# Two transformer layers on one core: the per-group convolution table built in one piece, and one call that prepares weights early taken out

## The reference, cut to what matters

```python
def _conv_ffn(x, w_up, conv_w, conv_b, w_down):
    u = x @ w_up
    val, gate = u[..., :D_FF], u[..., D_FF:]            # D_FF = 2816 = 22 * 128
    gp = jnp.pad(gate, ((0, 0), (CONV_WIDTH - 1, 0), (0, 0)))
    h = conv_b + sum(gp[:, j:j + s] * conv_w[j] for j in range(CONV_WIDTH))
    return (jax.nn.silu(h) * val) @ w_down

def s5_mixer(h, ..., d_skip, w_glu):
    ...
    y = lax.map(scan_sequence, u)                        # 64 groups of 16 channels
    y = y + d_skip.reshape(SSM_GROUPS, SSM_GROUP) * u
    ...
```

## Time and profile before

| | |
|---|---|
| runs | 1783.55, 1789.47, 1784.94 us; median 1784.94 |
| the profiled execution | 1783.55 us, its span 1781.7 us |
| mean granted clock of TensorE | 0.992 |
| PE busy | 97% of the span |
| DVE, ACT, POOL busy | 45%, 38%, 40% |

### The profile page before, as it was taken

How to read it: one execution, slowest core, us unless ns; L and a number is a source line. 1 busy time by engine, 2 the same in 40 slices (tenths; PEclk the granted TensorE clock), 3 DMA queues, 4 the chain that set the end, 5 groups by cost and what they waited for, 6 DMA issues and landing times.

```text
span 1781.7 us, 22762 instructions
## 1 busy us (share of the span) xinstructions
PE 1734.6 (97%) x9006; PEld 1443.6 (81%) x9006; DVE 793.9 (45%) x1430; ACT 673.9 (38%) x1176; POOL 710.7 (40%) x331
## 2 busy tenths in 40 slices
PE   8999999999999898999999999999999999999999
PEld 6887977788788687789888888888888888888887
DVE  3876899678756547333111111148664411111111
ACT  3333344244243656433322222266654333122221
POOL 5432344444444231434453434333801244344342
PEclk9999999999999899999999999999999999999999
DMA  9422224453535457214333333222101233333332
GB/s 245 97 79 83 72 87 153 136 150 121 151 112 168 133 205 253 92 59 119 95 96 100 94 101 95 79 80 82 54 1 33 75 107 95 95 95 95 100 96 77
DMA packets 241288, 189.61 MB, mean 106 GB/s; under 512 B 40480, under 2 KB 198304, under 8 KB 241184
## 3 DMA queue, kind: packets, MB, share of 16 engines
q1 hardware_dynamic: 239312, 182.79, 34.4%
q10 hardware_dynamic: 1872, 5.37, 0.9%
HBM read 168.73 MB, written 19.40 MB: 106 GB/s over the span
## 4 chain that ended last, share of the span: by engine, by line
PE 83%; DVE 10%; ACT 3%; issue 2%; DMA 1%; POOL 1%; DVEq 0%; SPq 0%; ACTq 0%
PE ps L372 12%; PE ps L374 12%; PE ps L373 12%; PE ps L398 10%; PE ps L399 10%; PE ps L400 10%; PE ps L429 3%; PE ps L431 3%; PE ps L430 3%; PE ps L874 2%; PE ps L855 2%; PE ps L865 1%; DVE x_rows L1681 1%; PE ps L847 1%; ACT w_hi L1163 1%
## 5 line engine op out<-in xcount | busy, mean ns | idle before, releaser
L1013 POOL TENSOR_TENSOR w_lo<-w_raw,w_hi 128x1024 fp32r<-128x1024 f32 (+3 forms) x283 | 674.3, 2395 | 1010.2 <-ACT w_hi L1163 1010.2
L372 PE MATMUL ps<-a_hi,w_hi 128*128 128x512 f32 (+1 forms) x1184 | 442.8, 374 | 3.0 <-DVE ev L2003 3.0
L373 PE MATMUL ps<-a_lo,w_hi 128*128 128x512 f32 (+1 forms) x1184 | 441.1, 373 | 0.0
L374 PE MATMUL ps<-a_hi,w_lo 128*128 128x512 f32 (+1 forms) x1184 | 441.0, 372 | 0.0
L1163 ACT ACTIVATE w_hi<-w_raw 128x1024 fp32r<-128x1024 f32 (+3 forms) x283 | 283.2, 1019 | 212.8 <-DMA w_raw<-in_ffn_w_gate_up_dram 71.1
L372 PEld LDWEIGHTS ps<-a_hi,w_hi 128*128 128x128 f32 x1184 | 223.4, 189 | 43.6 <-DVE ev L2003 3.2
L374 PEld LDWEIGHTS ps<-a_hi,w_lo 128*128 128x128 f32 x1184 | 223.4, 189 | 39.0
L373 PEld LDWEIGHTS ps<-a_lo,w_hi 128*128 128x128 f32 x1184 | 223.4, 189 | 38.5
L2146 DVE TENSOR_TENSOR ev<-ps,xh 128x512 f32<-128x512 f32 x44 | 30.4, 692 | 411.9 <-PE ps L374 382.9
L398 PE MATMUL ps<-w_hi,h_hi 128*128 128x512 f32 x476 | 190.5, 400 | 7.2 <-DVE ev L2003 4.0
L399 PE MATMUL ps<-w_lo,h_hi 128*128 128x512 f32 x476 | 189.5, 398 | 0.0
(11 more groups left out here) (345 smaller groups left out, 2335.9 us busy)
## 6 DMA issues: line engine op xcount, KB each, us to landing
w_raw<-in_ffn_w_gate_up_dram SPq DMA_DIRECT2D x88, 512.0 KB, 3.8
w_raw<-in_w_up_dram SPq DMA_DIRECT2D x44, 512.0 KB, 4.1
w_raw<-in_ffn_w_down_dram SPq DMA_DIRECT2D x40, 512.0 KB, 3.7
w_raw<-in_w_in_dram SPq DMA_DIRECT2D x20, 512.0 KB, 4.3
w_raw<-in_w_down_dram SPq DMA_DIRECT2D x20, 512.0 KB, 4.4
s_records<-stage SPq DMA_DIRECT2D x16, 544.0 KB, 5.3
w_raw<-in_ssm_w_glu_dram SPq DMA_DIRECT2D x16, 512.0 KB, 4.2
rec<-s_records SPq DMA_DIRECT2D x14, 544.0 KB, 5.3
```

The lines of the kernel that those rows point to most:

```text
L372: pe.matmul(bank, wh, xh_, start=first, stop=False)
L373: pe.matmul(bank, wh, xl_, start=False, stop=False)
L374: return pe.matmul(bank, wl, xh_, start=False, stop=last)
L1013: pool.tensor_tensor(w_lo[:, n % RING, 0:w], w_raw[:, n % RING, 0:w], w_hi[:, n % RING, 0:w].bitcast(F), ALU.subtract).then_inc(lo_made, 1)
```

## The change

Three things change.

1. The four small products of `prepare` go to partitions 0 to 15 of the bank, side by side in its 512 columns, in place of four places 32 partitions apart. ACT copies the whole of it to `k_s` with one instruction of 16x4x128, which now frees the bank. DVE waits for that, multiplies the identity with `d_skip` for four groups at once into a scratch tile (16x64), waits for itself, adds it to the first 16 columns of `k_s` (16x4x16), and waits for that too. The eight passes on PE stay eight.
2. `d_skip` is loaded in another layout: two DMAs of 16x64 single numbers in place of four of 16x16.
3. The call at L1259 is gone: ACT makes chunks only 4 ahead.

```diff
-N_CONST, N_TURNED, N_PARAM = 13, 8, 7
+N_CONST, N_TURNED, N_PARAM = 13, 8, 5
...
-                b = open_bank(("s5k", f), freed_by=(k_w, f + 1))
+                b = open_bank(("s5k", f))
                 for g in range(GB):
-                    m = pe.matmul(b[KQ * g:KQ * g + GK, 0:P], h_bs[f % 2][:, g, T - 1, :],
+                    m = pe.matmul(b[0:GK, g * P:g * P + P], h_bs[f % 2][:, g, T - 1, :],
                                   stages[f % 2][:, P_O + g * 144:P_O + g * 144 + P], start=True, stop=True)
...
-                    for g in range(GB):
-                        sp.dma_start(d_c[KQ * g:KQ * g + GK, :],
-                                     ssm_d_2[0].rearrange("(f g k) -> g k f", g=GB, k=GK)[g]).then_inc(p_in, 16)
+                    for o in (0, KQ):
+                        sp.dma_start(d_t[o:o + GK, :], ssm_d_2[0].rearrange("(g k) -> k g", g=G)).then_inc(p_in, 16)
...
-                b = full(act, ("s5k", f))
-                for g in range(GB):
-                    ins = act.activation(k_rows(f)[:, g, KPAD + GK:], b[KQ * g:KQ * g + GK, GK:P], ACT.Copy)
-                ins.then_inc(k_evicted, 1)
+                b = full(act, ("s5k", f))[0:GK, :].rearrange("p (g c) -> p g c", g=GB)
+                release(("s5k", f), act.activation(k_rows(f)[:, :, KPAD:], b, ACT.Copy))
...
                             act.activation(gconv[:, f % 2, :], b, ACT.Identity, scale=cw_c[:, 2, f:f + 1],
                                            bias=cb_c[:, f:f + 1]).then_inc(gate_pre, 1)
-                            make(chunks_at[(stage, "gate", f)] + RING)
                             act.wait_ge(gate_conv, f + 1)
...
             def s5_diagonal(f):
-
-                v.wait_ge(k_evicted, f + 1)
-                b = full(v, ("s5k", f))
-                for g in range(GB):
-                    at_g = slice(KQ * g, KQ * g + GK)
-                    ins = v.scalar_tensor_tensor(k_rows(f)[:, g, KPAD:KPAD + GK], ident[at_g, at_g], d_c[at_g, f:f + 1],
-                                                 b[at_g, 0:GK], ALU.mult, ALU.add)
-                ins.then_inc(k_w, 1)
+                v.wait_ge(*freed[bank_no[("s5k", f)]])
+                at_f = slice(KQ * (f % 2), KQ * (f % 2) + GK)
+                dk = tmp1[at_f, 0:GB * GK].rearrange("p (g c) -> p g c", g=GB)
+                step(v.tensor_tensor(dk, ident[at_f, at_f].unsqueeze(1).to_broadcast([GK, GB, GK]),
+                                     d_t[at_f, f * GB:f * GB + GB].unsqueeze(2).to_broadcast([GK, GB, GK]), ALU.mult))
+                o = k_rows(f)[:, :, KPAD:KPAD + GK]
+                v.tensor_tensor(o, o, dk, ALU.add).then_inc(k_w, 1)
+                v.wait_ge(k_w, f + 1)
```

More of the change, by code:

```diff
@@ L165, in program @@
         lam = scratch("lam", [P, 3, G], F, 86.5)
-        d_c = scratch("d_c", [P, NB], F, 61.5)
+        d_t = scratch("d_t", [KQ + GK, G], F, 61.5)
         stages = [scratch("stage0", [P, M_O], F, 41), scratch("stage1", [P, M_O], F, 32)]
@@ L288, in program @@
         e_w = sem("e_w")
-        k_evicted = sem("k_evicted")
         k_w = sem("k_w")
```

## The result

The changed kernel takes 1797.52 us, the median of five runs (1794.92 to 1798.27), against 1785.84 for the kernel before beside it: 11.7 us between the two medians. The ratio over all runs of the two is 1.0056, with a 95% interval of 1.0042 to 1.0070, which makes 10 us. It is slower. The prediction said 1786 with a range to 1793; the time lies above the range.

What follows compares the result with a forecast made beforehand. PE, busy for 97% of the span, was taken to bound the kernel. Passes +7.1, the wait at 454 us -3.5, the end at 582 us -0.3 and the first group -1.4 gave +1.9 on 1783.55: 1786 us, range 1779 to 1793.

Steps and rivals of the forecast that it cites:

- ACT's lead: First group without L1259: DVE meets fewer w_lo, but PE then waits for chunks made later; -1.4 us for the group.
- the diagonal's: First group: DVE's two new SBUF-only instructions could be held by w_lo, but nothing was added for it.
- Rival 1: Shorter lead delays PE at the first w_down chunk (304.4 us) and the clock may be lost at 454; 1793 us, chance 0.12.
- Passes, +0.65 us each, 1.05 us for eight: PE's eight passes per batch take 1.06 us instead of 0.41; 11 batches on the path, +7.1 us.
- The copy and the diagonal: ACT's copy falls from 1.05 to 0.60 us, DVE's diagonal from 0.95 to 0.5.
- Columns of the first group: PE waits for w_lo, 1.7 us near 226 and about 2 near 302, clock kept; w_down product starts at 302.0.
- The wait at 454: PE's wait for DVE's adds shrinks from 2.75 to 1.65 us and the clock is kept; -3.5 us.
- Second and third group 0: Shorter lead costs nothing there, since PE is the slowest engine and waits for nobody before 451 us.
- the loads 0: The d_skip DMAs may take some us longer, covered by 27 us before first need; zero.
- The end at 582 to 610: Chain of PE's last passes, ACT's copy, the diagonal and the add before the layer norm; -0.3 us.
- Against the profiled execution: The sum of +1.9 us was put on the profiled execution of 1783.55 us, giving 1785.5; 1786 for a median.

Runs made afterwards that it cites:

- e4_psum_diag: The changed kernel with the diagonal again four DVE instructions that read PSUM, on the side-by-side layout: 1799.24 us, ratio 1.0076.
- e11_new_diag: The kernel before with the new diagonal and the new loads, four strips and longer lead as before: 1784.39 us, ratio 0.9998.
- e2_s5k: The changed kernel with ACT's longer lead (the call at L1259) put back: 1793.71 us, ratio 1.0046.
- e1_lead: The kernel before with only the shorter lead of ACT (the call at L1259 removed): 1792.89 us, ratio 1.0043.
- e7_short_g12: The kernel before with the shorter lead in the second and third group alone: 1782.63 us, ratio 0.9985.
- e6_short_g0: The kernel before with the shorter lead in the first group alone: 1792.95 us, ratio 1.0041.

## Why the prediction was wrong

**The failed step is "ACT's lead", first group: "Until the `ev` of f = 6 (300.89), DVE meets two w_lo fewer (-4.1)."** They are fewer until then, but nothing removes them. ACT's next call asks for the same chunk with or without L1259, so the two are made behind the last Silu, from 310 us on, beside the tables. The step followed them to the start of the product with w_down (where "it eats the gain") and stopped there, with -1.4 us for the group. The next thing that PE needs from DVE is the adds. PE opens the four banks of the second half together, for which it needs the first two adds (where they are late, PE restarts 1.6 us after the first one starts, in four runs of four). Before, the second ended at 324.96, and PE came 1.9 us later:

```profile
326.87 0.40 PE L398 MATMUL ps<-w_hi,h_hi 128*128 128x512 f32 x1
```

Ahead of these adds stand six table instructions and a diagonal. I had not read that stretch of DVE. Measured from 316 to 339 us: +7.1 in the changed kernel where the forecast has +0.3, and +10.5 with the lead alone, a wait of 4.9 or 7.8 us and half speed behind it.

**A second term failed in the same place, the diagonal's: "I add nothing, since in the first group a pair of w_lo holds two DVE instructions whichever they are."** Beside the shorter lead that holds, since other instructions are held in the diagonal's place (e4_psum_diag is no faster than the changed kernel). With the longer lead it does not: the `w_lo` from 321.87 us on met the diagonal and the adds, which read PSUM and are not held, and the new diagonal put two instructions that read SBUF alone there, 4.3 us in that stretch (e11_new_diag). So putting the lead back in the changed kernel (e2_s5k) wins only 3.8 us; 3.5 us of the loss in that stretch stay, with a wait of 3.2.

No rival had the adds. Rival 1 named the right edit, but put the delay at 302 us (+2.5 and +1.5), by the supply of chunks, and had place, size and mechanism wrong.

The other steps:

- **Passes, +0.65 us each, 1.05 us for eight.** Right. Timeline of PE in the changed kernel, which answers to the earlier trace rows:

```profile
369.94 1.05 PE L651 MATMUL ps<-stage,h_b 128*16 128x128 f32 x8
```

  The forecast was 1.06. The four pairs above measure 6.9 us in all, against +7.1. The 1.64 us by the factor of the Trainium skill (TensorEngine Tiling (Array Packing), Theoretical Speedup) was too much: four strips measure 2.6 times the speed here, and the length of one pass, 0.28 us, is in both numbers.
- **The copy and the diagonal.** The copy takes 0.59 at 316.61 us, the diagonal 0.46 where no `w_lo` is near: both as forecast. Beside `w_lo` the diagonal takes up to 4.8. The Trainium skill (SBUF — State Buffer, SBUF: two separate sides) says that GpSimd and a DVE instruction with two SBUF inputs exclude each other; the trace agrees with 2.43 and 2.28 us for instructions that take 0.21. The prediction named this rule and priced it at nothing; see above.
- **Columns of the first group.** Right as far as it went. PE stands for `w_lo` at 226, 252, 277 and 302 us, 6.5 us in all, with the clock at full speed behind each, and the product with w_down starts at 303.7, or 302.3 without the 1.4 us that this execution was already late at 223. The forecast was 302.0. That the clock was kept at all four was in part luck: in e1_lead a wait of 2.24 us at 252 us lost it.
- **The wait at 454.** Right in sign, -1.4 against -2.2 for the stretch. The clock stays full, but PE first waits 1.1 us for a table (L1949), which the step did not have. With the longer lead the step comes out: e2_s5k waits 1.52 us for a forecast of 1.65, keeps the clock and has -2.2. The shorter lead gains here by itself, with neither longer passes nor shorter copies: e1_lead has -3.0.
- **Second and third group 0, the loads 0.** Right: e7_short_g12 is not slower, and e11_new_diag, with the new loads, is as before.
- **The end at 582 to 610**: +0.6 against -0.3, mis-sized by 0.9 us.
- **Against the profiled execution.** The prediction took that execution as typical of the rest of the program. It was a fast one: see the 3.6 us in the table's last row, and below.

## What to carry to other kernels

In this kernel, work that a shorter lead took out of one stretch was made in another: follow each deferred item to the place where it lands, and read there which engine it holds and what the bound engine needs from that one next. Where two engines exclude each other, a row of their instructions runs in turns, so put what others wait for ahead of such a row, not behind it. A sum that ends at the first new wait is not done; the slack of the next hand-over has to be read as well. And before an instruction that reads PSUM is rebuilt from SBUF operands, look what the other engine does beside it.

## What the runs showed of the hardware

**Taking turns costs more than being held once.** The prediction priced a pair of `w_lo` at 4.1 us of DVE. In e1_lead, where both engines have work queued, every DVE instruction with two SBUF inputs costs one `w_lo`: 2.8 to 2.9 us for 0.7, six times in a row, and POOL loses as well (2.8 us for 2.45).

**A wait of the same length may or may not cost the clock.** In the earlier trace rows PE waits 1.99 us for `w_lo`, and the clock behind it is at full speed. The same wait in the changed kernel, to the hundredth:

```profile
1189.66 0.37 PE L428 MATMUL ps<-w_hi,a_hi 128*128 128x288 f32 x1 [1.99 <-POOL w_lo L1012]
```

```profile
1190.00:1194.00 4.00, 4.00 (x21) 4.00 (x20) 1.29 (x2) 0.89 (x2) 1.84 (x1) 0.58 0.00 0
```

The clock is mostly at 1.2 GHz for 4 us, and it costs 1.5. Of 14 profiled executions of 14 kernels, 9 lose it there and 5 don't, the kernel before among these 5; at a wait of 1.7 us near 1263 us, 5 of 14 lose another 1.7. The other way round, the wait of 2.75 us of the earlier trace rows lost the clock, and one of 2.73 at the same place in e6_short_g0 kept it:

```profile
463.40 0.47 PE L398 MATMUL ps<-w_hi,h_hi 128*128 128x512 f32 x1 [2.73 <-DVE x_rows L1652]
```

```profile
463.00:466.00 3.00, 2.60 (x11) 2.18 (x12) 2.96 (x6) 1.06 (x1) 1.16 (x1) 1.00 0.96 318
```

So the one row from which the prediction took the clock as kept at waits under 2 us makes no rule: from 1.7 to 3.0 us both happen (3.00 at 227 us lost it in the kernel before, 2.99 near 301 kept it in e11_new_diag). What decides it stays open. It makes 1.5 to 3 us of chance between two profiled executions, and is a reason to take the size of an edit from a stretch of the trace and its sign from the medians.

**Small DVE instructions are quicker on one set of partitions.** The four of a diagonal take 0.94 us on PSUM partitions 0, 32, 64 and 96, and 0.65 where all four read partitions 0 to 15 (e4_psum_diag):

```profile
348.96 0.65 DVE L1959 SCALAR_TENSOR_TENSOR k_s<-ident,d_t,ps 16x16 f32<-16x16 f32 x4 [6.22 <-ACT k_s L1228]
```

Their start-to-start distance falls from 0.24 to 0.14 us. Besides PSUM, the identity and `d_skip` were read on four sets of partitions before and on one here; which operand makes the difference was not tried.
